# A hybrid decoder layer on one core: the order of low halves, bank emptying and state copies in the mixer loop

## The reference, cut to what matters

```python
h = rmsnorm(x, lw['g_mix'])
proj = h @ lw['w_in']                     # 1024 -> 10272 columns
u, lru_buf = causal_dwconv(lru_in, lru_buf0, lw['lru_conv_w'], lw['lru_conv_b'])
hs, lru_h = rg_lru(u, lru_h0, ...)        # gates by two 128x128 blocks, then a scan over time
y_a = hs * jax.nn.gelu(lru_gate)
xbc_c, ssd_buf = causal_dwconv(xbc, ssd_buf0, lw['ssd_conv_w'], lw['ssd_conv_b'])
xbc_c = jax.nn.silu(xbc_c)                # split into xs, B, C
y_ssd, ssd_s = ssd_chunked(xs, dt, A, Bm, Cm, ssd_s0)
y_b = grouped_rmsnorm((y_ssd + D * xs) * jax.nn.silu(z), lw['ssd_norm_g'], SSD_GROUPS)
merged = sigmoid(gate_a) * (y_a @ w_br_lru) + sigmoid(gate_b) * (y_b @ w_br_ssd)
x = x + merged @ lw['w_out']
```

## Time and profile before

| what | value |
|---|---|
| timed runs | 1002.57, 1008.92, 1009.87 us, median 1008.92 |
| profiled execution | 1002.44 us, of it a span of 1000.6 us from the first instruction to the last |
| mean granted clock of TensorE over the span | 0.94 |
| PE / PEld busy | 899.4 us (90%) / 681.3 us (68%) |
| DVE / ACT / POOL busy | 585.7 us (59%) / 414.8 us (41%) / 168.3 us (17%) |
| matmuls of L1465, L1466, L1467, 640 each | 203.9, 196.0, 195.1 us |
| `whi`, L722, 82 of them | 86.9 us, 1060 ns each |
| `wlo`, L1008, 82 of them | 108.0 us, 1318 ns each |
| chain that ended last | PE 59%, DVE 17%, issue 12%, ACT 7%, POOL 2% |

### The profile page before, as it was taken

The page is one execution under the profiler, slowest core; times in us unless marked ns, Lnnn a source line. Parts: engine busy times, 40 slices in busy tenths (PEclk is TensorE's granted clock), DMA queues, the critical chain, the costliest instruction groups (busy, mean ns, idle before and its releaser), DMA issues.

```text
span 1000.6 us, 16530 instructions
## 1 busy us (share of the span) xinstructions
PE 899.4 (90%) x5345; PEld 681.3 (68%) x5345; DVE 585.7 (59%) x1092; ACT 414.8 (41%) x713; POOL 168.3 (17%) x214
## 2 busy tenths in 40 slices
PE   6589999989889998998969999989999999999986
PEld 3388879878787887888849997774444444444464
DVE  2786777788787778878785542434333242423534
ACT  2457565655746565465764321351111111111232
POOL 0045233241513324152400000020000000000000
PEclk9889898989979898999959999998999999999998
DMA  7154462727346272734637513935999999999201
GB/s 202 43 134 127 112 179 63 194 74 204 81 117 179 54 204 69 199 84 126 173 108 198 165 39 109 385 148 193 382 391 380 383 388 392 379 389 376 65 1 47
DMA packets 208603, 188.54 MB, mean 188 GB/s; under 512 B 8000, under 2 KB 166392, under 8 KB 208568
## 3 DMA queue, kind: packets, MB, share of 16 engines
q1 hardware_dynamic: 207352, 187.12, 58.5%
q10 hardware_dynamic: 1216, 0.98, 0.4%
HBM read 176.88 MB, written 11.21 MB: 188 GB/s over the span
## 4 chain that ended last, share of the span: by engine, by line
PE 59%; DVE 17%; issue 12%; ACT 7%; POOL 2%; DVEq 1%; DMA 1%; POOLq 0%; SPq 0%; ACTq 0%
PE bank L1768 12%; PE bank L1796 6%; PE bank L1724 6%; PE bank L1632 5%; PE bank L1731 4%; PE bank L1465 3%; PE bank L1661 3%; PE bank L1467 3%; PE bank L1466 3%; PE bank L1816 3%; PE bank L1636 2%; DVE wlo L1008 2%; DVE cv L1075 2%; PE bank L1538 2%; DVE arena L1193 1%
## 5 line engine op out<-in xcount | busy, mean ns | idle before, releaser
L1465 PE MATMUL bank<-h_hi,whi 128*128 128x288 f32 x640 | 203.9, 319 | 20.8 <-DVE wlo L1008 20.6
L1466 PE MATMUL bank<-h_lo,whi 128*128 128x288 f32 x640 | 196.0, 306 | 0.0
L1467 PE MATMUL bank<-h_hi,wlo 128*128 128x288 f32 x640 | 195.1, 305 | 0.0
L1465 PEld LDWEIGHTS bank<-h_hi,whi 128*128 128x128 f32 x640 | 127.6, 199 | 32.4 <-DVE wlo L1008 27.2
L1362 DVE TENSOR_TENSOR xT<-xT,bank 128x288 f32<-128x288 f32 x128 | 49.6, 449 | 152.3 <-PE bank L1731 152.3
L1466 PEld LDWEIGHTS bank<-h_lo,whi 128*128 128x128 f32 x640 | 127.6, 199 | 1.0
L1467 PEld LDWEIGHTS bank<-h_hi,wlo 128*128 128x128 f32 x640 | 127.4, 199 | 0.0
L722 ACT ACTIVATE whi<-wb 128x1024 fp32r<-128x1024 f32 x82 | 86.9, 1060 | 91.1 <-PE bank L1467 79.2
L1008 DVE TENSOR_TENSOR wlo<-wb,whi 128x1024 fp32r<-128x1024 f32 x82 | 108.0, 1318 | 23.0 <-ACT whi L722 16.0
L936 ACT ACTIVATE Gs<-bank 128x512 f32<-128x512 f32 x16 | 9.6, 597 | 144.8 <-PE bank L1768 144.8
L1724 PE MATMUL bank<-pick,htok 96*128 96x256 f32 x240 | 59.0, 386 | 1.1 <-ACT yb L915 1.1
(11 more groups left out here) (368 smaller groups left out, 1564.9 us busy)
## 6 DMA issues: line engine op xcount, KB each, us to landing
wb<-in_w SPq DMA_DIRECT2D x80, 1024.0 KB, 8.4
wb<-in_w_in SPq DMA_DIRECT2D x80, 512.0 KB, 4.0
wb3a<-in_w SPq DMA_DIRECT2D x16, 1024.0 KB, 8.6
arena<-in_state_ssd SPq DMA_DIRECT2D x16, 512.0 KB, 5.7
out_new_ssd_s<-arena SPq DMA_DIRECT2D x16, 512.0 KB, 5.9
wb<-in_w_br_ssd SPq DMA_DIRECT2D x16, 512.0 KB, 3.9
wb<-in_w_br_lru SPq DMA_DIRECT2D x8, 512.0 KB, 4.0
wb<-in_w_out SPq DMA_DIRECT2D x8, 512.0 KB, 4.0
```

Source lines behind the costliest of these rows:

```text
L1465: mm(bP[i % 2][:, 0:T], hi, h_hi[:, k, :], start=(k == 0), stop=False)
L1466: mm(bP[i % 2][:, 0:T], hi, h_lo[:, k, :], start=False, stop=False)
L1467: ins = mm(bP[i % 2][:, 0:T], lo, h_hi[:, k, :], start=False, stop=(k == KC - 1))
```

## The change

Lines change places in three parts of the mixer's group; no instruction is added, removed or resized. On DVE low halves 4, 5 and 6 stand ahead of convolutions 1, 2 and 3 instead of behind them. On ACT `evac` of blocks 3 and 4 (high halves 5 and 6, and the emptying of the two banks) stands ahead of silus 1 and 2; `from_T(4)`, the copy into `sprev`, ahead of `decay_rows(2)` and so ahead of the root; `from_T(8)` ahead of `evac(g, 10)`.

```diff
@@ block.scalar, group(g, first, last)
                 evac(g, 2)
+                evac(g, 3)
                 silu(1)
-                evac(g, 3)
+                evac(g, 4)
                 silu(2)
-                evac(g, 4)
                 silu(3)
@@
                 raw(8, ga[:, ds(g, 1), :].rearrange("p o t -> p (o t)"))
+                from_T(4, sprev[:], 256)
                 decay_rows(2)
                 decay(2)
@@
                 if not first:
                     root(g)
-                from_T(4, sprev[:], 256)
                 from_T(5, sT[:, 0:4, :].rearrange("p b n -> p (b n)"), 512)
                 from_T(6, sT[:, 4:8, :].rearrange("p b n -> p (b n)"), 512)
                 raw(9, gb[:, ds(g, 1), :].rearrange("p o t -> p (o t)"))
                 from_T(7, sT[:, 0:4, :].rearrange("p b n -> p (b n)"), 512)
+                from_T(8, sT[:, 4:8, :].rearrange("p b n -> p (b n)"), 512)
                 if not last:
                     evac(g, 10)
-                from_T(8, sT[:, 4:8, :].rearrange("p b n -> p (b n)"), 512)
@@ block.vector, group(g, first, last)
+                small(g, 4)
                 conv(g, 1, C_SW, 32, C_SB, 2 * g + 1)
-                small(g, 4)
+                small(g, 5)
                 conv(g, 2, C_SW, 32, C_SB, g + 16)
-                small(g, 5)
+                small(g, 6)
                 conv(g, 3, C_SW, 32, C_SB, g + 24)
-                small(g, 6)
                 conv(g, 4, C_LW, 8, C_LB, g)
```

## The result

| what | before | after |
|---|---|---|
| timed runs, median (lowest to highest) | 1009.39 (1002.57 to 1010.95) us | 1036.01 (1034.57 to 1040.22) us |
| profiled execution / its span | 1002.4 / 1000.6 us | 1040.2 / 1038.4 us |
| end of the mixer's last projection | 493.74 us | 528.24 us |

The changed kernel takes 1.0313 times as long, 95% interval 1.0282 to 1.0345. On the forecast's base of 1008.92 us that is 1040 (1037.4 to 1043.7), outside the range of 1009 to 1037. The two medians alone give 1.026, and 1036.0 us by itself lies just inside the range. Slower was right, by how much was not: a rise of 19 us, from 1009 to 1028, was forecast, and 27 (by the medians) to 32 (by the ratio) were measured. Of the 37.8 us between the two profiled executions 34.5 lie in the mixer and 3.3 behind it, where nothing was changed.

What follows compares the result with a forecast made beforehand. It held that DVE and ACT bound the mixer's turn as much as PE. Terms 9.1+12.0-3.6+5 = +22.5 us on the profiled 1002.4 gave 1025, plus half the spread 1028 us; range 1009 to 1037.

Steps and rivals of the forecast that it cites:

- What bounds the kernel: Mixer loop, 58.6 us a turn: DVE and ACT set it as much as PE, which arrives last by only 0.4 us.
- the signs named: Expected trace: L1557 waits 2 to 3 us, both L1096 long, low 11 over 2 us, scan 0.76, turn 60 to 61.
- Low halves ahead of convolutions: Start of a group on DVE: fourth silu later, +0.95 us in groups 2, 3, 5, 6; +9.1 us over all groups.
- L+0.15: Assumed start of low half 4, 0.15 us after convolution 1's old start L; L-0.4 was the estimated earliest.
- s + 11.9: Predicted end of the fourth silu, 11.9 us after low half 4's start s, behind three low halves and convolutions.
- Banks: ACT empties banks 3 and 4 ahead of silus 1 and 2: nothing gained or lost by itself.
- State copy ahead of the root: Copy into sprev makes the root 0.33 us later and DVE second to POOL: +2.0 us a group, +12 in six.
- the hold: Behind the root, POOL's L680 and L645 delay DVE's norm rows and low 11; the scan is then free.
- State copy ahead of a high half: Last L781 ahead of high half 12 shortens DVE's waits at L1197: -2.6 us in group 0, -3.6 in all.
- The clock: Projection 6 at the lower clock every other time after 3.0 us of PE idleness: +5 us, bounds 0 and +12.
- the clock falls in every group: Rival: lower clock in all eight groups, +12 us for it, +29.5 in all; 1032, 1035 with half spread; chance 0.18.
- the fourth rival: Nothing moves: early losses in the turn are repaid by later slack, 1003 to 1009 us; chance 0.06.

Runs made afterwards that it cites:

- e7: Kernel before with only banks 3 and 4 emptied ahead of silus 1 and 2: 1009.0 us, ratio 1.0032.
- e6: Kernel before with only low halves 4 to 6 moved ahead of the convolutions, banks left as before: 1077.7 us, ratio 1.0692.
- e11: Kernel before with from_T(8) moved and POOL's Dg made later, after an added wait, beside DVE instructions reading PSUM: 997.6 us, ratio 0.9895.
- e3: Kernel before with only from_T(8) moved ahead of high half 12: 1002.8 us, ratio 0.9956.
- e2: Kernel before with only the copy into sprev moved ahead of the root: 1012.5 us, ratio 1.0066.
- e8: Kernel before with from_T(8) moved and POOL's Dg placed behind the first copy of last columns: 1011.4 us, ratio 1.0057.
- e1: Kernel before with low halves and banks moved, both state copies left in place: 1041.2 us, ratio 1.0365.
- e5: Changed kernel with the sprev copy put back behind the root: 1033.4 us, ratio 1.0275 to the kernel before.
- e9: The changed kernel timed again, unaltered: 1035.8 us, ratio 1.0285 to the kernel before.
- e4: Changed kernel with 18 unused matmuls filling PE's idleness ahead of L1557: 1020.8 us, ratio 1.0157 to the kernel before.
- e10: Changed kernel with 18 unused matmuls ahead of L1557 and the sprev copy put back: 1009.9 us, ratio 1.0044 to the kernel before.

## Why the prediction was right and wrong

**What bounds the kernel: right.** More than half of the waits of the earlier trace rows went, and the kernel got slower; DVE's order, the held instructions and the clock behind the new wait set the turn. Of the signs named, L1557's wait (3.1 us), both L1096, low 11 and the scan came as told; the turn, 62.4 and 63.9 us instead of 60 to 61, did not.

**Low halves ahead of convolutions: right, 1.9 us too much.** Low 4 starts 0.6 us behind the tail where the high half is there in time, which is the early end of the bounds given (L-0.4), not the L+0.15 taken. Behind it the count held: the fourth silu ends at conv 1 + 10.76, and the sum's s + 11.9 is the same number. So +0.6 us a clean turn, not +0.95. Group 1 lost +0.9 instead of +2.2, group 4 gained 0.3, group 0 lost 2.7 instead of 1.9.

**Banks: right as a term, incomplete as a reason.** "Nothing gained or lost by itself" is e7, at 1.0032 (1.0006 to 1.0057). What wasn't said is that without them the moved low halves would make the fourth silu 3.8 us later in each turn (e6).

**State copy ahead of the root: right in size and mechanism.** +0.33 us at the root was measured as +0.33, and the hold at +1.66 where the sum had +1.67 (2.0 with the root's part in it). The second L1096 ended at 347.66 + 1.74 = 349.40, 0.32 us after the pair of L680 (345.08 + 4.00 = 349.08), and low 11 at 355.54, 1.08 us after L645's end at 354.46, where the sum had about that. The Trainium skill (SBUF — State Buffer, Who interferes with whom) has the second to issue blocked fully. The trace agrees in that the held instruction ends only behind the other; but by that rule alone the norm row would need its own 0.52 us behind that end, and it needed 0.32, as the prediction had taken from the earlier trace rows. The same section has it that a DVE instruction with at most one input in SBUF does not contend; e11 agrees, with L1194 at 1.41 us for two beside a POOL instruction of 2.11 us.

**State copy ahead of a high half: right in size, its cause shared.** -3.2 for -3.6; e3 alone gained 2.5. But e2 shows that the earlier copy into `sprev` takes the same waits away without this move.

**The clock: wrong, and this is the step that failed.** "After 3.0 us I expect it every other time" rested on waits of another length: the 1.8 us ahead of projection 4, which were followed by the lower level in one group of before and not in three others. For that length every other time is about right: over before, e2, e3, e7, e8 and e11 projection 4 ran at the lower level behind 12 of 26 waits of 1.7 to 1.8 us. The new idleness is longer, and the lower level followed in eight groups of eight; over all five kernels with moved low halves and no filling (changed kernel, e1, e5, e6, e9) projection 6 lost clock in 39 groups of 40, behind 2.3 to 5.4 us. The price for each was too low as well. Group 4 of before gave 1.4 us of loss for one projection. Measured were 1.6 us in four groups and 3.0 to 3.1 in the other four, in which the lower clock had begun within 0.8 us of L1557's start and covered most of what runs up to the end of projection 6. Together that is 18.5 us, 2.3 a group, where the sum had 5 and its upper bound 12. e4 shows that it is the clock and not the wait: the silu just as late, PE kept busy, and 15 us came back. That bound was no bound, since it multiplied the worst count by a middle price. With 18.5 in its place the sum is 36, for the 34.5 measured. The rival "the clock falls in every group" had the count right, and its 1035 us is close to the 1036.0 of the median; part of that is luck, since its +12 for the clock was 6.5 too little, its order of low halves 1.9 too much, and the half spread added to it was a guess.

**Terms that don't add.** The sum treated the start of the turn, the clock and the hold as independent. e5 shows they aren't: 12 us less of hold gave 2.6, because a DVE that comes sooner meets high half 4 behind projection 2, and because the stretches of lower clock then fall elsewhere. That it is the length of the turn that moves them is argued, not shown. Some are hidden (projection 1), some are not (projection 6, projection 0 ahead of L1197). With the clock held up the terms nearly add: e4 to e10 gave 10.9. Why the lower clock sometimes begins ahead of L1557's work and sometimes only at projection 6, so that turns of 62.4 and 63.9 us alternate, stays open: no experiment moved it alone. In e9, the same kernel, the two lengths stand in the other groups.

**The base.** Half the spread was added to get from the profiled execution to a median. The changed kernel's own profile was its slowest run, 4 us above its median. This uncertainty is as large as some of the terms. The stated range, from 1009, also left out the fourth rival (1003 to 1009), which the prediction doesn't say.

## What to carry to other kernels

Before moving work to remove an engine's waits, ask which engine the next meeting point will wait for, and by how much; here PE came last by 0.4 us, so a move that helps PE and adds 1.1 us ahead of the end of DVE's part can only lose at that point. Price a new idle stretch of PE by its length and by what runs next: a wait of 3 us cost 1.6 to 3.1 more in the work behind it, and cheap unused matmuls in the gap showed it. Where two engines hold one another up and one is first by less than 0.1 us, a delay of 0.3 us turned them round; what helped was to place the long instruction beside ones with an input in PSUM, as e11 did.

## What the runs showed of the hardware that was not expected

- Idle stretches of PE of 2.4 to 3.1 us ahead of L1557 were followed by the lower clock in all eight groups of the changed kernel, at a cost of 1.6 or 3.1 us; one of 2.42 us, in e5, was not. Cut to 1.04 us or less by unused matmuls, they were followed by it once in sixteen groups (e4, e10).
- A held DVE instruction does not need its whole duration once it is let go: 0.32 us of 0.52 for a norm row, 1.08 of 1.23 for a low half.
- The hold reaches the scan and the scalar-tensor-tensor form as well as tensor-tensor: 2.35 us instead of 0.76 and 1.98 instead of 0.52, each beside one POOL instruction of 2.0 to 2.1 us.
